# Decoder block with product-key experts on one core: 48 in place of 64 gathered tokens of the second tile, three u buffers, a four-slot ring for the late v loads

## The reference, cut to what matters

```python
q = (xb @ w_q).reshape(TOK_BLOCK, PK_HEADS, 2, D_HALF)
s = jnp.einsum('thcd,hcnd->thcn', q, subkeys)
...            # top 16 of 128 keys twice, top 16 of the 256 sums: idx, softmax g
a = jax.nn.gelu(jnp.einsum('td,thkd->thk', xb, u[idx]), approximate=False)
w = g * a
return jnp.einsum('thk,thkd->td', w, v[idx])
```

## Time and profile before

| | us |
|---|---|
| median of three runs | 1586.9 |
| lowest, highest | 1579.42, 1588.41 |
| the profiled execution's own time | 1582.95 |
| its span in the profile | 1581.2 |
| PE busy | 1525.8 (96%) |
| DVE, ACT, POOL busy | 1311.8, 696.5, 860.6 |

### The profile page before, as it was taken

The page is one execution under the profiler, slowest core; times in us unless marked ns, Lnnn a source line. Parts: engine busy times, 40 slices in busy tenths (PEclk is TensorE's granted clock), DMA queues, the critical chain, the costliest instruction groups (busy, mean ns, idle before and its releaser), DMA issues.

```text
span 1581.2 us, 25858 instructions
## 1 busy us (share of the span) xinstructions
PE 1525.8 (96%) x9474; PEld 1346.2 (85%) x9474; DVE 1311.8 (83%) x2648; ACT 696.5 (44%) x1021; POOL 860.6 (54%) x530
## 2 busy tenths in 40 slices
PE   9999999999998989888999999999999999999988
PEld 8987877888888979888988899998999988777767
DVE  5898675746899989898857988898988988888886
ACT  6333566444343446566753334333343333333334
POOL 4675444334556777777624665655655554544430
PEclk9999999999999999999999999999999999999999
DMA  5332223453223679999888999999999999999984
GB/s 159 97 93 81 67 67 103 125 146 121 81 94 116 218 261 346 330 340 321 281 270 314 382 373 361 368 374 363 363 371 353 370 331 345 321 335 332 348 327 143
DMA packets 156538, 402.86 MB, mean 255 GB/s; under 512 B 12448, under 2 KB 62112, under 8 KB 156320
## 3 DMA queue, kind: packets, MB, share of 16 engines
q1 hardware_dynamic: 59328, 203.13, 36.4%
q0 software_dynamic: 46080, 167.79, 28.6%
q10 hardware_dynamic: 51040, 30.82, 6.8%
HBM read 371.81 MB, written 28.84 MB: 253 GB/s over the span
## 4 chain that ended last, share of the span: by engine, by line
PE 51%; DMA 18%; DVE 13%; POOL 8%; issue 6%; ACT 3%; ACTq 0%; SPq 0%; DVEq 0%; POOLq 0%
PE ps L2293 14%; PE ps L2148 13%; DMA vraw<-in_v 9%; PE ps L1827 6%; PE ps L1890 5%; DMA rows<-in_u,gidx_x 5%; POOL uwlo L674 4%; DMA uraw<-in_uT 3%; PE ps L2054 3%; DVE vwlo L1631 2%; DVE acc L1666 2%; POOL wlo L602 2%; DVE rows L1581 2%; ACT vwhi L1048 2%; PE ps L2067 1%
## 5 line engine op out<-in xcount | busy, mean ns | idle before, releaser
L2148 PE MATMUL ps<-hThi,uwhi 128*128 128x320 f32 x1024 | 307.8, 314 | 8.2 <-ACT act L1033 8.1
L1048 ACT ACTIVATE vwhi<-vraw 128x1024 fp32r<-128x1024 f32 x128 | 135.8, 1061 | 401.8 <-PE ps L2293 212.0
L2148 PE MATMUL ps<-hTlo,uwhi 128*128 128x320 f32 x1024 | 305.2, 311 | 0.0
L714 POOL DMA_INDIRECT rows<-in_v,gidx x128 | 190.2, 1486 | 188.2 <-DVE acc L1666 173.6
L714 POOL DMA_INDIRECT rows<-in_u,gidx x128 | 192.9, 1507 | 156.3 <-DVE rows L1659 108.0
L1000 ACT ACTIVATE uwhi<-uraw 128x1024 fp32r<-128x1024 f32 x127 | 134.4, 1059 | 189.6 <-DMA uraw<-in_uT 105.6
L1631 DVE TENSOR_TENSOR vwlo<-vraw,vwhi 128x1024 fp32r<-128x1024 f32 x128 | 156.5, 1223 | 68.6 <-ACT vwhi L1048 68.2
L674 POOL TENSOR_TENSOR uwlo<-uraw,uwhi 128x1024 fp32r<-128x1024 f32 x66 | 160.8, 2436 | 91.4 <-ACT uwhi L1000 58.3
L2148 PEld LDWEIGHTS ps<-hThi,uwhi 128*128 128x128 f32 x1024 | 193.8, 189 | 11.6 <-ACT uwhi L1000 8.1
L2148 PEld LDWEIGHTS ps<-hTlo,uwhi 128*128 128x128 f32 x1024 | 193.8, 189 | 1.2
L2293 PE MATMUL ps<-vwhi,awhi 128*128 128x512 f32 x720 | 185.0, 392 | 7.6 <-ACT awhi L1053 7.5
(11 more groups left out here) (382 smaller groups left out, 3083.0 us busy)
## 6 DMA issues: line engine op xcount, KB each, us to landing
vraw<-in_v SPq DMA_DIRECT2D x128, 512.0 KB, 6.0
uraw<-in_uT SPq DMA_DIRECT2D x127, 512.0 KB, 5.1
raw<-in_wstream SPq DMA_DIRECT2D x70, 512.0 KB, 3.5
gmat<-gates_dram SPq DMA_DIRECT2D x64, 384.0 KB, 7.1
gates_dram<-piece ACTq DMA_DIRECT2D x11, 2048.0 KB, 17.2
xt<-in_xT SPq DMA_DIRECT2D x8, 264.0 KB, 5.3
acc<-in_x ACTq DMA_DIRECT2D x4, 512.0 KB, 4.7
rows<-in_u,gidx POOLq DMA_INDIRECT x128, 7.6
```

The source lines that it names most:

```text
L714: pool.indirect_dma_start(out=rows[n % SLOTS][:], out_offset=None, in_=u if q < P else v, in_offset=bass.IndirectOffsetOnAxis(ap=gidx[:, q ...
L1048: act.activation(vw["hi"][:, m % 2, :], vraw[:, m % 2, :], ACT.Copy).then_inc(S["v_hi"], 1)
L2148: ins = pe.matmul(ps[:, k, 0:UCOLS], u_weights(a, k, far)[:, c * P:(c + 1) * P], hT[b][:, c, P + EXTRA:TOK], start=i == 0, stop=i == len(U ...
```

## The change

It alters a set of numbers together, and the code that they need.

- EXTRA is 48 in place of 64: one piece of 32 tokens (WIDE) and one of 16 (NARROW). UCOLS is 336. Three pieces have 16 tokens, ten have 32, thirteen in all where there were twelve; a narrow one is written in runs of 256 B where the wide ones have 512 B. The sixteen gathered tokens of the narrow piece lie on half the partitions, so their indices and sums are moved between partitions by two sets of four small DMAs from ACT's queue, and `ynat_x` takes twelve DMAs (four of 128 KB, eight of 64 KB).
- `uraw` has three buffers. The u blocks n = 0 to 127 are all loaded by number (the one that went through `vraw` is gone).
- From v block V_LATE = 68 on, when u is over, v loads go round four buffers: two of `vraw` and two of `uraw`.
- LAG is 64 (64 kept activations, 64 pairs, 64 single v blocks), U_TOP 26, U_FILL 30, X_FILL 3, NMAIN 42. The places of the search products, of the exponentials and of the early gathers are moved accordingly.
- The gates of the gathered tokens are copied by ACT (`known_gates`, two small copies for each v block) in place of one copy on DVE. The loads of `gmat` wait for `aw_hi` in place of `prod_ok`. For eight stores of the kept activations the Gelu is two instructions.
- ACT's wait for the stored pieces before the first v block now takes in the last piece, since that one lies where the v weights go.

```diff
-EXTRA = 2 * GT
+WIDE, NARROW = GT, GT // 2
+EXTRA = WIDE + NARROW
 UCOLS = DENSE - EXTRA
+WIDTHS = [WIDE, NARROW, NARROW] + [GT] * (NPIECE - 2)
+PIECES = [*range(2, len(WIDTHS)), 0, 1]
-U_TOP = 24
-LAG = 70
-U_FILL = 36
-X_FILL = 4
+U_TOP = 26
+LAG = 64
+U_FILL = 30
+X_FILL = 3
+U_RAWS = 3
+V_RAWS = 4
+V_LATE = NPAIR + 4
-SUMS_POS, SUMS_I, SUMS_J = (8, 16), (9, 18), (13, 21)
+SUMS_POS, SUMS_I, SUMS_J = (10, 17), (11, 19), (14, 20)
-EARLY_X = {16: 2, 17: 4, 19: 6, 20: 8, 22: 10, 23: 12, 24: 14}
-ITEMS_X = (4, 8, 12)
+EARLY_X = {18: 2, 19: 4, 20: 6, 22: 8, 23: 10, 24: 12, 26: 14}
+ITEMS_X = (2, 6, 10)
-    return min(ITEMS, ITEMS_FIRST + (47 * min(m, NPAIR) + 21 * max(m - NPAIR, 0) + 15) // 16)
+    return min(ITEMS, ITEMS_FIRST + (45 * min(m, NPAIR) + 20 * max(m - NPAIR, 0) + 15) // 16)
...
+            def next_u(n):
+
+                need(sp, S["u_lo"], n - U_RAWS + 1)
+                sp.dma_start(u_raw(n), uT[n]).then_inc(u_in[n % U_RAWS], 16)
...
+                    sp.wait_ge(S["v_lo"], V_LATE - 1 if m < V_LATE + 2 else V_LATE if m < V_LATE + 4 else m - V_RAWS + 1)
+                    if m in (V_LATE + 1, V_LATE + 3):
+                        sp.wait_ge(S["u_lo"], NK)
+                    sp.dma_start(v_raw(m), v[m * P:(m + 1) * P]).then_inc(v_late[(m - V_LATE) % V_RAWS], 16)
...
-            for x_ in range(XP):
-                for g in range(QUAD):
-                    act.dma_start(ynat_x[g * GT:(g + 1) * GT, x_, :], ynat[x_ * GT:(x_ + 1) * GT, 1, :]).then_inc(S["ynx_in"], 16)
+            for g in range(QUAD):
+                act.dma_start(ynat_x[g * GT:(g + 1) * GT, 0, :], ynat[0:WIDE, 1, :]).then_inc(S["ynx_in"], 16)
+            for g in range(2 * QUAD):
+                act.dma_start(ynat_x[g * NARROW:(g + 1) * NARROW, 1, :], ynat[WIDE:EXTRA, 1, :]).then_inc(S["ynx_in"], 16)
...
+            def known_gates(m):
+
+                if m == 0:
+                    act.wait_ge(g_store[1], 16 * (len(PIECES) // 2))
+                if m % GRP == 0:
+                    act.wait_ge(gm_in[m // GRP % 2], m // GRP // 2 * 32 + 32)
+                need(act, S["aw_ok"], m - 1)
+                for c in range(2):
+                    act.activation(prod[:, m % 2, FIRSTS[c]:FIRSTS[c + 1]], gates_of(m, c), ACT.Copy).then_inc(S["x_ok"], 1)
...
                 if n == LAG - 2:
-                    act.wait_ge(g_store[0], 16 * NPIECE // 2)
+                    act.wait_ge(g_store[0], 16 * (len(PIECES) // 2 + 1))
                     v_split(0)
```

More of the change, by code:

```diff
@@ L82 @@
 PB = GT // BATCH
-EXTRA = 2 * GT
-XP = EXTRA // GT
+WIDE, NARROW = GT, GT // 2
+EXTRA = WIDE + NARROW
 UCOLS = DENSE - EXTRA
-UP = UCOLS // GT
 QUAD = P // GT
-PIECES = [*range(XP, NPIECE), *range(XP)]
+WIDTHS = [WIDE, NARROW, NARROW] + [GT] * (NPIECE - 2)
+FIRSTS = [sum(WIDTHS[:c]) for c in range(len(WIDTHS))]
+PIECES = [*range(2, len(WIDTHS)), 0, 1]
+MAIN = FIRSTS[3]
 NBATCH = DENSE // BATCH
@@ L197, in batches_ahead, with piece_of @@
     return next(b for b in range(NBATCH + 1) if filled(b) >= PRODUCTS * (n - U_TOP))
+def piece_of(batch):
+    first = batch_tokens(batch)
+    c = max(c for c in range(len(WIDTHS)) if FIRSTS[c] <= first)
+    return PIECES.index(c), (first - FIRSTS[c]) // BATCH
 def batch_tokens(batch):
@@ L400, in in_pieces, with gates_of, main_gates @@
[L400 to L405, removed]
+        def gates_of(m, c):
+            wide, first = WIDTHS[c], FIRSTS[c] * GRP + m % GRP * WIDTHS[c]
+            return gmat[:, m // GRP % 2, first:first + wide]
+        def main_gates(m):
+            return gmat[:, m // GRP % 2, MAIN * GRP:DENSE * GRP].rearrange("p (c i t) -> p c i t", i=GRP, t=GT)[:, :, m % GRP, :]
@@ L421, in build, with kept @@
+        stores += [act1[:, i] for i in range(20)] + [act3[1][:]]
+        stores += [act0[:, i] for i in range(14, 20)]
+        stores += [act3[i][:] for i in (2, 3)]
+        assert len(stores) == LAG
+        def kept(n):
+            store = stores[n % LAG]
+            if n % LAG in HOLE_STORES:
+                cut = (UCOLS - NARROW) // 2
+                return store[:, :, cut:], store[:, :, 0:cut]
+            return store[:, 0:NARROW], store[:, NARROW:]
         ps = ctx.enter_context(nc.psum_tensor("ps", [P, 8, 512], F32))
@@ L500, in _, with next_gates @@
+            def next_gates(g, half):
+                need(sp, S["aw_hi"], (g - 1) * GRP)
+                own = slice(half * GRP * DENSE // 2, (half + 1) * GRP * DENSE // 2)
+                sp.dma_start(gmat[:, g % 2, own], gates_dram[g, :, own]).then_inc(gm_in[g % 2], 16)
+            next_u(2)
             for k in range(2):
                 sp.wait_ge(S["w_lo"], N_TILES - 1 + k)
[L502 to L516, removed]
-            def next_gates(g, half):
-                need(sp, S["prod_ok"], (g - 1) * GRP)
-                own = slice(half * NPIECE // 2, (half + 1) * NPIECE // 2)
-                sp.dma_start(gmat[:, g % 2, own].rearrange("p c i t -> p (c i t)"),
-                             gates_dram[g, :, own.start * GRP * GT:own.stop * GRP * GT]).then_inc(gm_in[g % 2], 16)
@@ L1086, in gates_out @@
             def gates_out(batch):
-                o, s = batch // PB, batch % PB
+                o, s = piece_of(batch)
                 c = PIECES[o]
+                dst = (slim if WIDTHS[c] == NARROW else piece)[o % 2]
                 for q in range(2):
@@ L1580, in item_x @@
                 dve.wait_ge(row_in[q % SLOTS], q // SLOTS * 16 + 16)
-                dve.scalar_tensor_tensor(out=row[:], in0=row[:], scalar=1.0, in1=ynat_x[:, q // GT, :], op0=ALU.mult,
+                dve.scalar_tensor_tensor(out=row[:], in0=row[:], scalar=1.0, in1=ynat_x[:, int(q in NARROW_X), :], op0=ALU.mult,
                                          op1=ALU.mult, accum_out=dots_x[:, q:q + 1]).then_inc(S["item_ok"], 1)
```

204 lines of the change are left out of this document (125 added, 79 removed).

## The result

The changed kernel takes 1560.8 us (median of 4 runs, 1559.4 to 1562.5), the kernel before 1585.9 beside it: a ratio of 0.985, 95% interval 0.982 to 0.988. Forecast were 1571 us and a range of 1556 to 1592. The profiled execution has a span of 1560.5 us, 20.7 less than that of before; forecast were 13 less.

A forecast was written before the change was run, and what follows sets the result against it. PE was taken to bound the pair stage; in the one-hot stage three nearly full engines wait for one another. Terms 1 - 31 - 3 + 56 - 37 + 1 = -13 us gave 1570 to 1574, stated as 1571, range 1556 to 1592.

The forecast's parts named there:

- the pace falls to the floor: Rival: one-hot batches at 4.15 us and search stage at its lower bound, -25 us in all, 1559; chance 20%.
- the forecast case: The prediction's own sum: -13 us in all, given as 1571 us; chance 45%.
- One-hot pace: One-hot stage: 38 main batches at 4.35 us each instead of 5.27; the stage 201.7 us for 232.9, -31.
- Load and buffer depth both improve: One-hot stage: reason given for 4.35 us a batch, a little above the floor, though three engines stay nearly full.
- Columns: u matmuls of 336 columns for 320: 153.4 ns for 146.7, 0.16 us more a block, +20.7 us over 128 blocks.
- v alone: v blocks after the pairs: 64 x 4.09 + 8 = 269.8 us, -37; 24.5 from six blocks moved into pairs.
- the ring: Four buffers for late v loads behind the pairs: the stall of 13 us goes, 8 of 21 us are left.
- Layout DMAs: Search stage: four more ynat_x issues on ACT, 0.66 us each, put +2.6 us on the path, or 0 if priced by bytes.
- late first gathers: Search stage: first gathers stand two uwlo later, some 4 to 5 us; first gate product +1 us, bounds -3 and +8.
- After the gates: Last gate product to first v product: 6.5 u blocks instead of 7.5, 30.2 us before, -3 us.
- The slow store: Rival: last store's 256 B packets cost double, 19.6 us, ACT 8 us later; sum -5, 1579; chance 7%.
- a doubled price of each packet: Last store: if each 256 B packet costs double, 19.6 us instead of 9.8, and the sum becomes -5.

The follow-up runs named there:

- the experiment: Changed kernel with every v block, the last ones too, going through two v buffers instead of the late ring of four: 1565.9 us, ratio 0.991.
- the last experiment: Changed kernel with layout DMAs spread over key blocks, first gathers two lo parts earlier, last store's second part issued from SP: 1547.2 us, ratio 0.979.
- the spread DMAs alone: Changed kernel with ACT's twelve layout DMAs (ynat_x) spread behind the first eight key blocks instead of in one row: 1551.0 us, ratio 0.980.

## Why the prediction was right, and where it was off

Faster, and inside the range. But the time is nearer to the rival "the pace falls to the floor" (1559) than to the forecast case, and some terms came out right for other reasons.

- *One-hot pace.* Forecast 4.35, "a little above the floor" of 4.13; measured 4.18, with VectorE busy all the time, and its part of 14 items given back costs 16 us. This term is most of the miss of 8 us (20.7 for 13): 38 x 0.17 = 6.5. The last ten batches took 34.6 us for 36.4.
- *Why the pace fell.* "Load and buffer depth both improve" stands, and no part does it alone. From the changed kernel's side: third buffer 0.12, one gather less in advance 0.11, VectorE's items 0.35 a batch. From the side of before: 14 items 0.06, eight blocks fewer 0.17, both 0.41, of 1.09 in all. Like executions differ by 0.08, so the small ones are rough. I hadn't seen the lead of the gathers. Four row buffers hold 2.8 batches of 1.44 items, or four batches of one; from issue to item were 9.4 us before (39 items from 580 to 725 us, landing after 7.4) and 13.3 after (35 items). The kernels with left-out items kept their places in this order, so they didn't gain the lead: from issue to item are 9.0 us with 36 blocks and 9.6 with 28. The last of these stands at 4.86, the kernel with three gathers and two u loads ahead at 4.41. Most of these 0.45 us is VectorE waiting for rows: 16.9 us in 155 (0.53 a batch) against the 6.4 above (0.18).

```profile
DVE rows L1596 <- DMA rows<-in_u,gidx_x: 16.9, 10, 4.3
```

Why rows are late more often there, at the same 9.6 us from issue to item, stays open, and so does the part of PE's lower clock (0.94 for 0.98).

- *Columns.* The price of 0.16 us a block held for the first 64 blocks (153.3 ns a matmul, forecast 153.4) and not for the 64 from block 64 on, which cost 0.225 (156.0 ns). The line through three sizes was right; that later blocks could be slower was not in the sum. In the pairs this adds 63 x 0.065 = 4 us, of which the table shows half (+58.0 for +56), since the kernel before stood some 2 us over PE's pace there (57 pairs of 7.615 us are 434.1 of its 435.9). By the blocks alone the columns cost 24.6 us; 19 to 22 came back without them, because those beside VectorE's batches hide theirs. That this is near the forecast total of 20.7 is luck.
- *v alone.* -40.9 for -37. The 271.0 us hold 65 v blocks, 265.2 us at PE's pace, so 5.8 us are over it where 8 were kept; before it was 21.5 (71 blocks, 290.4 of 311.9). Of the 13 us put down to the ring the experiment shows 5 to 9; in the kernel before the ring gives 10. With two buffers v blocks of the changed kernel came 4.10 us apart in one execution, and 4.29 in another with 21 items in 16 blocks. A load begins at the end of the lo part two blocks back; load to hi 5.77, hi to the end of lo 2.80, together 8.6 us for two blocks before (50 blocks from 1310 to 1525 us), against 5.61 and 2.62 in that execution. PE needs 8.16. So it lies at an edge, and the ring takes it off; what decides between 4.10 and 4.29 is not shown.
- *Layout DMAs.* Forecast +2.6, and PE's wait did go from 2.6 to 5.24 us. But the lower clock behind it was not in the sum: the first u matmul came 4.7 us later (457.7 to 462.4). That is more than the +3.8 at the first gate product. The late first gathers, for which the forecast kept 1 us, cost too: VectorE waits 4.02 us for them, and with them two lo parts earlier, in the last experiment, the first gate product stands 2.9 us earlier than with the spread DMAs alone (567.2 to 564.3).
- *After the gates.* -2.4 for -3. PE waits 2.2 us for ScalarE, which the store's issue holds for 4.3 us, below; the sum had no such term, but the kernel before has waits of 2.26 and 0.95 us in this stretch.
- *The slow store.* The rival didn't occur: the split of v starts at 786.09, right behind a Gelu and 17 us after the store's first issue. (There are two narrow pieces and eleven wide ones, 2 x 16 + 11 x 32 = 384 tokens, not three and ten as said ahead of the prediction.) In the last kernel, where landings are recorded, the whole narrow piece took from its first issue at 756.86 to the last landing at 757.14 + 10.0 us, 10.3 us for 1 MB; the wide one of before, of as many runs and twice the bytes, took 10.2 (804.76 to 805.16 + 9.8). So the whole piece took its time by packets. The first parts, of 1536 runs each, don't fit that as well: 8.6 and 9.4 us with 256 B, 5.1 with 512 B, beside other traffic. The Trainium skill (DMA: Bandwidth & Descriptors, Specifications) has a transfer reach line rate only from 512 B, and transfers below it read, modified and written. Half the bytes in the same time agrees with the first; a doubled price of each packet, my estimate in the prediction, would make some 20 us, and the whole piece doesn't show it.

## What to carry to other kernels

Count for each buffer not only how many there are but how much time they span: four rows at one item a batch of 4.18 us reach 17 us ahead, at 1.44 items a batch of 5.27 only 15. Measured from issue to item that was 13.3 us for 9.4, where a gather lands after 7.4; one row less cost 0.11 us a batch. Where three engines wait for one another, taking load from one can give little by itself (0.06 and 0.17 us a batch, both 0.41); test a cause from both kernels. And put DMA issues into the idle time of their engine: twelve moved issues gave 7 to 10 us, beside some 24 for the whole change.

## What the runs showed of the hardware

- *A stall costs more than its length.* Behind PE's wait of 5.24 us the granted clock was 0.51 in 359 to 363 us (about the lower level, 1.2 GHz) and 0.64 in 363 to 367; matmuls of 256 columns stood 0.21 us apart instead of 0.12. Behind the 2.6 us of before it stayed 1.00 (360 to 370 us).

```profile
359.00:363.00 4.00, 3.09 (x14) 3.09 (x15) 3.10 (x3) 0.77 (x2) 0.85 (x1) 0.51 0.44 125
363.00:367.00 4.00, 4.00 (x25) 4.00 (x24) 1.38 (x2) 1.19 (x2) 0.00 (x0) 0.64 0.47 200
```

- *A DMA behind a store in short runs waits in the issuing queue.* The first part of the last store is issued in 0.37 us; the next holds ScalarE's queue for 4.30 us (1.69 in the kernel before, whose runs are 512 B). Issued from SP instead, the store itself takes 1.22 us, and the load behind it 6.08. The stores before and after differ in the length of their runs and not in their number; that the length is the cause is argued from these rows alone:

```profile
769.25 0.37 ACTq L1157 DMA_DIRECT2D gates_dram<-slim  x1
769.64 4.30 ACTq L1158 DMA_DIRECT2D gates_dram<-slim  x1
```

```profile
757.14 1.22 SPq L564 DMA_DIRECT2D gates_dram<-slim  x1
758.40 6.08 SPq L537 DMA_DIRECT2D vraw<-in_v  x1
```

- *The same matmul can have two paces at the full clock.* 256 columns: 120 ns, 320: 146.7, 512: 227.2, 0.42 ns a column. 336 columns: 153.3 in the first 64 u blocks, on that line, and 156.0 in the last 64, every fifth being 163. In the kernel with 320 of them the halves have 147.0 and 146.6. Why is open.
- *An item takes 3.40 us instead of 1.22 beside GpSimd's subtraction*, and ends 1.1 us after that does. The Trainium skill (SBUF — State Buffer, "Who interferes with whom") calls the port pair that the two share an exclusive lock, and has a VectorE instruction with two SBUF inputs contend with a GpSimd one that reads SBUF; these rows of the changed kernel agree:

```profile
764.29 1.22 DVE L1739 SCALAR_TENSOR_TENSOR rows<-rows,ynat 128x1024 f32<-128x1024 f32 x1
764.38 3.37 POOL L701 TENSOR_TENSOR uwlo<-uraw,uwhi 128x1024 fp32r<-128x1024 f32 x1 [4.17 <-ACT uwhi L1027]
...
765.43 3.40 DVE L1739 SCALAR_TENSOR_TENSOR rows<-rows,ynat 128x1024 f32<-128x1024 f32 x1
```
